# A feed-forward stage: sums of the activations made from a kept scaled input, and the seven-product form begun one hidden tile earlier

## The reference

```python
def rms_norm(x):
    xf = x.astype(jnp.float32)
    return (xf * lax.rsqrt(jnp.mean(xf * xf, -1, keepdims=True) + RMS_EPS)).astype(x.dtype)

def swiglu(h, w_in, w_out):
    gate, up = jnp.split(h @ w_in, 2, axis=-1)
    return (jax.nn.silu(gate) * up) @ w_out
...
        h2 = rms_norm(x) * (1 + sc2) + sh2
        x = x + g2 * swiglu(h2, w_ffn_in[i], w_ffn_out[i])
```

## Time and profile before

| | |
|---|---|
| median of three runs | 2867.03 us |
| the profiled execution | 2864.24 us |
| its span, first to last instruction | 2862.4 us |
| TensorE busy | 2773.7 us, 97% of the span |
| VectorE, ScalarE, GpSimd busy | 1547.7, 918.8, 952.4 us |
| feed-forward from the end of tile 1 | 2192.9 us to the end |
| granted TensorE clock, mean | 0.993 of full |

### The profile page before, as it was taken

How to read it: one execution, slowest core, us unless ns; L and a number is a source line. 1 busy time by engine, 2 the same in 40 slices (tenths; PEclk the granted TensorE clock), 3 DMA queues, 4 the chain that set the end, 5 groups by cost and what they waited for, 6 DMA issues and landing times.

```text
span 2862.4 us, 60609 instructions
## 1 busy us (share of the span) xinstructions
PE 2773.7 (97%) x25599; PEld 2316.0 (81%) x25599; DVE 1547.7 (54%) x1682; ACT 918.8 (32%) x1380; POOL 952.4 (33%) x667
## 2 busy tenths in 40 slices
PE   5999999999999999999999999999998899999999
PEld 4797979898988888887877777888886688888887
DVE  5655555545454646477875666566657633333333
ACT  5312121313131313145454777111122232233322
POOL 1403040404030303044442111333336565566652
PEclk9999999999999999999999999999998999999999
DMA  6202020202020201043331212466311112112122
GB/s 213 67 21 60 21 67 13 75 6 77 3 77 13 67 18 53 18 144 112 121 92 49 60 51 69 149 214 196 114 48 44 30 55 63 45 44 60 50 62 80
DMA packets 224700, 201.93 MB, mean 71 GB/s; under 512 B 22370, under 2 KB 193468, under 8 KB 224444
## 3 DMA queue, kind: packets, MB, share of 16 engines
q1 hardware_dynamic: 210976, 150.70, 17.7%
q10 hardware_dynamic: 13467, 47.31, 4.7%
HBM read 167.57 MB, written 30.41 MB: 69 GB/s over the span
## 4 chain that ended last, share of the span: by engine, by line
PE 91%; DVE 3%; POOL 2%; issue 2%; ACT 2%; DMA 1%; SPq 0%; ACTq 0%; POOLq 0%; DVEq 0%
PE ps L295 67%; PE ps L1052 3%; PE ps L1066 3%; PE ps L1063 2%; PE ps L1030 2%; PE ps L1115 1%; PE ps L1252 1%; PE ps L1277 1%; PE ps L1020 1%; PE ps L1265 1%; PE ps L986 1%; PE ps L1089 1%; PE ps L1099 1%; PE ps L1118 1%; PE ps L1072 1%
## 5 line engine op out<-in xcount | busy, mean ns | idle before, releaser
L295 PE MATMUL ps<-x_hi,w_hi 128*128 128x512 f32 (+1 forms) x2240 | 751.7, 399 | 15.1 <-ACT arena L1953 13.1
L295 PE MATMUL ps<-x_lo,w_hi 128*128 128x512 f32 (+1 forms) x2240 | 733.5, 391 | 0.0
L295 PE MATMUL ps<-x_hi,w_lo 128*128 128x512 f32 (+1 forms) x2240 | 733.5, 391 | 0.0
L285 POOL CAST w_hi<-w_raw 128x1024 fp32r<-128x1024 f32 (+2 forms) x163 | 152.0, 933 | 1532.1 <-PE ps L295 1291.4
L295 PEld LDWEIGHTS ps<-x_hi,w_hi 128*128 128x128 f32 (+1 forms) x2240 | 413.7, 188 | 118.8 <-issue 20.7
L295 PEld LDWEIGHTS ps<-x_hi,w_lo 128*128 128x128 f32 (+1 forms) x2240 | 420.2, 188 | 91.4
L295 PEld LDWEIGHTS ps<-x_lo,w_hi 128*128 128x128 f32 (+1 forms) x2240 | 420.7, 188 | 87.7
L287 POOL TENSOR_TENSOR w_lo<-w_raw,w_hi 128x1024 fp32r<-128x1024 f32 (+2 forms) x163 | 335.4, 2058 | 13.0
L295 PE MATMUL ps<-hid,w_hi 128*128 128x512 f32 (+1 forms) x928 | 259.3, 399 | 12.5 <-DVE arena L2614 9.5
L295 PEld LDWEIGHTS ps<-hid,w_hi 128*128 128x128 f32 (+1 forms) x928 | 172.4, 190 | 56.8 <-issue 12.7
L2614 DVE SCALAR_TENSOR_TENSOR arena<-ps,mod,arena 128x1024 f32<-128x1024 f32 x88 | 112.8, 1284 | 122.1 <-PE ps L295 122.0
(11 more groups left out here) (329 smaller groups left out, 4262.9 us busy)
## 6 DMA issues: line engine op xcount, KB each, us to landing
w_raw<-in_w_in SPq DMA_DIRECT2D x78, 512.0 KB, 3.9
arena<-in_w_ada SPq DMA_DIRECT2D x48, 512.0 KB, 5.9
w_raw<-in_w_ffn_in SPq DMA_DIRECT2D x44, 512.0 KB, 3.8
arena<-gates_sig ACTq DMA_DIRECT2D x40, 512.0 KB, 4.2
gates_sig<-arena ACTq DMA_DIRECT2D x24, 512.0 KB, 2.7
w_raw<-in_w_ffn_out SPq DMA_DIRECT2D x22, 512.0 KB, 3.8
arena<-in_x SPq DMA_DIRECT2D x16, 512.0 KB, 6.5
y_a<-arena ACTq DMA_DIRECT2D x10, 512.0 KB, 2.6
```

What stands on the lines that cost most here:

```text
L285: nc.gpsimd.tensor_copy(hi, raw).then_inc(s_whi, 1)
L295: ins = nc.tensor.matmul(dst[h], wp, xp[h], start=first and m == 0, stop=last and m == 2, skip_group_check=on)
```

## The change

- `normed` writes all eight channel blocks of the scaled input into `mix` (free by then), which is kept whole, where a two-slot buffer was used in turn. VectorE no longer waits for the slot.
- The sums T1 to T4 are made by VectorE from this kept float32 input, one operation each per channel block (16 operations of 512 elements, in place; the shift `sh2` is added or taken off as a per-channel scalar in the same operation). GpSimd's `x_sum` and VectorE's two- and three-operation forms are gone. The low parts are written over the raw sums (`x_sums` is now a list of 33 places of 512, of which 16 lie on `mix`).
- `FIRST_FAST` is 2: tile 2 takes the seven-product form, and down 0 the piece form. Their weight blocks are no longer split whole by GpSimd; their pieces are split by ScalarE and GpSimd as for all later tiles.
- The first fast tile now waits for the sums one product at a time.
- ScalarE makes the Silu of tile 1 after the high parts of T1 and T2, then two of T3, then pieces 0 to 3 and two of T4; the rest stands behind its first copy out of PSUM (`among_first_snaps`). VectorE makes all 16 sums, ten low parts, and then the hidden product of tile 1.

```diff
-          ("wout0", 4, 2), ("wout1", 4, 2), ("ffn_first", 1, 2), ("ffn", 1, 6)]
+          ("wout0", 4, 2), ("wout1", 4, 2), ("ffn_first", 1, 2), ("ffn", 1, 2)]
...
-FIRST_FAST = 3
+FIRST_FAST = 2
 DOWNS = FF // P // FF_GROUP
-ITEMS = [item for i in range(1, DOWNS - 1) for item in (("up", 2 * i + 1), ("up", 2 * i + 2), ("down", i))]
+ITEMS = [("up", 2), ("down", 0)]
+ITEMS += [item for i in range(1, DOWNS - 1) for item in (("up", 2 * i + 1), ("up", 2 * i + 2), ("down", i))]
...
-        x_sums = sb("x_sums", [P, 3, 2, 4, 512], F32R)
+        x_sums = sb("x_sums", [P, 33, 512], F32R)
...
+        X_HI = {X_T1: (20, 21, 22, 23), X_T2: (16, 17, 18, 19), X_T3: (27, 32, 8, 10)}
+        X_LO = {X_T1: (1, 3, 5, 7), X_T2: (9, 11, 13, 15), X_T3: (0, 2, 4, 6)}
...
-            return (0 if q % 2 == 0 else 3), 1, 2
+            gate, other = 2 * SLOT_A, 2 - 2 * SLOT_A
+            return (gate, gate + 1, other) if q % 2 == 0 else (other + 1, gate + 1, other)
...
-            for k in range(4):
-                x_sum(k)
-                split_block(pool, Block("ffn", 2 + k), 1024)
...
-            pool.wait_ge(m_hl, upto(2))
+            pool.wait_ge(m_act, upto(1))
...
             up(Block("ffn", 0), Block("ffn", 1), 1, ready=(m_nh, 0, 1))
-            up(Block("ffn", 2), Block("ffn", 3), 2)
-            down("ffn", 4, 0, 0)
...
                 if q == 0:
-                    pe.wait_ge(m_sil, upto(3))
-                    pe.wait_ge(m_act, upto(3))
+                    pe.wait_ge(m_sil, upto(2))
                 pe.wait_ge(f_h, late(f_h, 2 * (q - 2) + 1))
                 half_product(r0, lambda k: x_quarter(0, k, 0), b1, True)
                 pe.wait_ge(f_post, late(f_post, 3 * (q - 1) + 1))
                 half_product(r0 + 1, lambda k: x_quarter(1, k, 0), d, True)
                 pe.wait_ge(f_snap, late(f_snap, 3 * q + 1))
                 if q == 0:
-                    pe.wait_ge(c_lo, late(c_lo, 12))
+                    pe.wait_ge(c_lo, late(c_lo, 4))
                 half_product(r0 + 2, x_sum_of(X_T2), b1, False)
                 pe.wait_ge(f_post, late(f_post, 3 * (q - 1) + 3))
+                if q == 0:
+                    pe.wait_ge(m_act, upto(2))
+                    pe.wait_ge(c_lo, late(c_lo, 8))
                 half_product(r0 + 3, x_sum_of(X_T1), c, True)
                 pe.wait_ge(f_snap, late(f_snap, 3 * q + 2))
+                if q == 0:
+                    pe.wait_ge(c_lo, late(c_lo, 14))
                 half_product(r0 + 4, x_sum_of(X_T3), b1, False)
...
-            x_sum_high(0)
-            x_sum_high(1)
+            for which in (X_T1, X_T2):
+                for k in range(4):
+                    x_sum_high(which, k)
             hidden(Block("ffn", 0), 1, 1)
-            hidden_high(1, 1)
-            x_sum_high(2)
-            x_sum_high(3)
-            hidden(Block("ffn", 2), 2, 0)
-            last_sum_high(0)
-            last_sum_high(1)
+            for k in range(2):
+                x_sum_high(X_T3, k)
             piece_high(0)
             piece_high(1)
-            last_sum_high(2)
-            last_sum_high(3)
-            act.wait_ge(s_dense, upto(Block("ffn", 5).before + 1))
-            hidden_high(2, 0)
             piece_high(2)
             piece_high(3)
+            for k in range(2):
+                last_sum_high(k)
+
+            def among_first_snaps():
+
+                hidden_high(1, 1)
+                for k in range(2, 4):
+                    x_sum_high(X_T3, k)
+                for k in range(2, 4):
+                    last_sum_high(k)
...
                         if q == 0:
-                            act.wait_ge(m_act, upto(3))
-                            act.wait_ge(c_lo, late(c_lo, 12))
+                            act.wait_ge(m_act, upto(2))
                         else:
                             act.wait_ge(f_h, late(f_h, 2 * q - (1 if j == 0 else 0)))
                         fn({0: s_p1, 2: s_u2, 3: s_p5}[j], ps[:, c if j == 3 else b1, :], ACT.Copy).then_inc(f_snap, 1)
+                        if q == 0 and j == 0:
+                            among_first_snaps()
...
-                    if k >= 1:
-                        dve.wait_ge(m_nh, upto(k))
...
+            def x_sum(which, k):
+
+                n11, n12, n21, n22 = (x_scaled(*q) for q in ((0, k, 0), (0, k, 1), (1, k, 0), (1, k, 1)))
+                sh_0, sh_1 = (mod[:, MOD_SH2 + 4 * h + k:MOD_SH2 + 4 * h + k + 1] for h in range(2))
+                if which == X_T1:
+                    dve.wait_ge(m_nh, upto(KT))
+                    v.tensor_tensor(n12, n12, n11, ALU.subtract).then_inc(c_d, 1)
+                elif which == X_T2:
+                    dve.wait_ge(c_d, late(c_d, k + 1))
+                    v.scalar_tensor_tensor(n22, n22, sh_1, n12, ALU.add, ALU.subtract).then_inc(c_d, 1)
+                elif which == X_T3:
+                    dve.wait_ge(c_d, late(c_d, 4 + k + 1))
+                    v.scalar_tensor_tensor(n11, n22, sh_0, n11, ALU.subtract, ALU.subtract).then_inc(c_d, 1)
+                else:
+                    v.scalar_tensor_tensor(n21, n21, sh_1, n22, ALU.add, ALU.subtract).then_inc(c_d, 1)
+
+            def x_sum_low(which, k, made):
+
+                raw, hi, lo = raw_place(X_LO[which][k]), x_sums[:, X_HI[which][k], :], x_sums[:, X_LO[which][k], :]
+                dve.wait_ge(c_d, late(c_d, ALL_SUMS))
+                dve.wait_ge(c_hi, late(c_hi, made))
+                v.tensor_tensor(lo, raw, hi.bitcast(F32), ALU.subtract).then_inc(c_lo, 1)
...
+            X_T4 = 3
             hidden_low(0, 0)
-            x_sum_low(0)
-            x_sum_low(1)
+            for which in (X_T1, X_T2, X_T3, X_T4):
+                for k in range(4):
+                    x_sum(which, k)
+            for k in range(4):
+                x_sum_low(X_T2, k, 4 + k + 1)
+            for k in range(4):
+                x_sum_low(X_T1, k, k + 1)
+            for k in range(2):
+                x_sum_low(X_T3, k, 8 + k + 1)
             product(Block("ffn", 1), 1, 1)
+            for k in range(2):
+                last_sum_low(k, 10 + k + 1)
             hidden_low(1, 1)
-            x_sum_low(2)
-            x_sum_low(3)
-            product(Block("ffn", 3), 2, 0)
...
+            for k in range(2, 4):
+                x_sum_low(X_T3, k, 12 + k - 1)
+            for k in range(2, 4):
+                last_sum_low(k, 14 + k - 1)
```

More of the change, by code:

```diff
@@ L523, in build @@
         s_fw = [counted_on(s_lw, PAIRS * 96), counted_on(s_mask, 16)]
-        SLOT_A = Block("ffn", 4).slot
+        SLOT_A = Block("ffn", 0).slot
         raw_a, raw_b = w_raw[:, SLOT_A, :], w_raw[:, 1 - SLOT_A, :]
@@ L753, in _ @@
                     if n == 0:
-                        sp.wait_ge(s_wsplit, upto(Block("ffn", 4 + part).before + 1))
+                        sp.wait_ge(s_wsplit, upto(Block("ffn", part).before + 1))
                     elif ITEMS[n - 1][0] == "up":
@@ L1469, in x_sum_of @@
             def x_sum_of(which):
-                return lambda k: (x_sums[:, which, 0, k, :], x_sums[:, which, 1, k, :])
+                return lambda k: (x_sums[:, X_HI[which][k], :], x_sums[:, X_LO[which][k], :])
             def fast_up(tile):
@@ L1956, in hidden_high, with x_sum_high @@
                 act.wait_ge(m_act, upto(tile + 1))
-                fn(hid_hi[:, t, :], ft[:, t, :], ACT.Copy).then_inc(m_hh, 1)
+                fn(hid_hi[:, t, :], hsum, ACT.Copy).then_inc(m_hh, 1)
             hidden_high(0, 0)
-            def x_sum_high(k):
-                act.wait_ge(c_pl, late(c_pl, 6 * k + 3))
-                fn(x_sums[:, X_T1, 0, k, :], raw_t1, ACT.Copy).then_inc(c_hi, 1)
-                act.wait_ge(c_d, late(c_d, 2 * k + 2))
-                fn(x_sums[:, X_T2, 0, k, :], raw_t2, ACT.Copy).then_inc(c_hi, 1)
-                act.wait_ge(c_pl, late(c_pl, 6 * k + 6))
-                fn(x_sums[:, X_T3, 0, k, :], raw_t3, ACT.Copy).then_inc(c_hi, 1)
+            def x_sum_high(which, k):
+                act.wait_ge(c_d, late(c_d, 4 * which + k + 1))
+                if which == X_T3 and k >= 2:
+                    act.wait_ge(c_lo, late(c_lo, 10 + k - 1))
+                fn(x_sums[:, X_HI[which][k], :], raw_place(X_LO[which][k]), ACT.Copy).then_inc(c_hi, 1)
             def last_sum_high(k):
-                act.wait_ge(c_d, late(c_d, 8 + 3 * k + 3))
-                fn(x_quarter(0, k, 1)[0], raw_t4[k % 2], ACT.Copy).then_inc(c_hi, 1)
+                act.wait_ge(c_d, late(c_d, 12 + k + 1))
+                act.wait_ge(s_dense, upto(Block("ffn", 1).before + 1))
+                fn(x_quarter(0, k, 1)[0], x_scaled(1, k, 0), ACT.Copy).then_inc(c_hi, 1)
             def piece_high(r):
@@ L2633, in last_sum @@
-            def last_sum(k):
-                h21, l21 = (t.bitcast(F32) for t in x_quarter(1, k, 0))
-                t2h, t2l = (x_sums[:, X_T2, part, k, :].bitcast(F32) for part in range(2))
-                t = raw_t4[k % 2]
-                n = 8 + 3 * k
```

(10 more changed lines are left out.)

99 lines of the change are left out of this document (16 added, 83 removed).

## The result

| | before | after |
|---|---|---|
| median of 4 runs each, same chip (us) | 2867.04 (2865.82 to 2869.16) | 2846.89 (2843.4 to 2849.4) |
| ratio of the medians, with its 95% interval | | 0.9928 [0.9911, 0.9945] |
| profiled execution: time, span (us) | 2864.24, 2862.4 | 2846.58, 2844.6 |
| mean granted clock of TensorE | 0.993 | 0.997 |

What follows compares the result with a forecast made beforehand. TensorE bounds the kernel, busy 2773.7 of 2862.4 us. End of tile 1 to down 1 takes 92.7 for 112.35, plus 0.6 from tile 1: 20.2 less, 2844.0; with 2.8 for the median, 2846 (range 2838 to 2855).

Steps and rivals of the forecast that it cites:

- twelve matmuls fewer: In tile 2, on TensorE's path: 12 matmuls at 0.2267 us each save 2.7 us, held for certain.
- slot wait: end of tile 1 earlier: VectorE's wait for a slot of `normed` goes, taking 0.6 us off the end of tile 1 (bounds 0 and 1.2).
- a sum, start to start: Each of VectorE's sixteen 512-wide sums takes 0.60 us; upper bound one turn with GpSimd, 1.7.
- end of tile 1's product: VectorE's hidden product of tile 1, behind all 16 sums and ten low parts, ends at 2208.4.
- waits for pieces (half products 1, 2): In tile 2, TensorE waits for GpSimd's low parts of A11 and A12: 1.0 and 0.6 us.
- wait for the copy (half product 3): In tile 2, TensorE idles 9.7 us for ScalarE's copy of a bank, which waits for tile 1's hidden product.
- slow matmuls behind it: In tile 2 behind the copy's wait, 1.7 us lost to the lower clock.
- wait ahead of half product 5: In tile 2, TensorE waits 0.4 us for the second copy, which ends at 2216.7.
- down 0; tiles 3 and 4: Down 0 runs as down 1, 21.76 us, without its 9.5 us of waits; tiles 3 and 4 as 5 and 6, 38.45.
- the short chain: Rival, chance 0.18: VectorE hardly meets GpSimd, 26 operations at 0.60 us ahead of the product; 27 us less, 2840.
- the stall would only have moved: Rival, 0.04 with "not what it says": tile 1's late product makes new waits 28 us or more; 2861 to 2867.
- the kernel become slower: Rival, chance 0.03: VectorE's 26 operations ahead of tile 1's product average over 1.7 us; at 1.95, 2873.

Runs made afterwards that it cites:

- e7: Changed kernel with four more 512-wide VectorE additions ahead of the product of tile 1; tile 2 took 35.95 us against 33.52, single run 2847.01 us.

## Why the prediction was right

2846.0 was forecast and 2846.89 measured. By its own steps (us, measured in the profiled execution):

| step | predicted | measured |
|---|---|---|
| twelve matmuls fewer | 2.7 | 2.7 |
| slot wait: end of tile 1 earlier | 0.6 | 0.2 to 0.3 |
| end of tile 1 | 2192.3 | 2193.11 |
| a sum, start to start | 0.60 | 0.60 (T1), 0.66 (with a scalar) |
| end of tile 1's product | 2208.4 | 2209.40 |
| waits for pieces (half products 1, 2) | 1.0 + 0.6 | 2.65 + 0.41 |
| wait for the copy (half product 3) | 9.7 | 7.84 |
| slow matmuls behind it | 1.7 | 2.5 |
| wait ahead of half product 5 | 0.4 | 0.22 |
| down 0; tiles 3 and 4 | 21.76; 38.45 | 21.76; 38.42 |
| end of tile 1 to down 1 | 92.7 | 93.70 |

**The mechanism held.** Silu is no longer waited for, the wait moved to the product of tile 1 and the copy behind it (lengthened by just what is added to VectorE's list), down 0 has no wait, and twelve matmuls are gone. The long wait is ended by the very chain that was forecast. The rivals fell: VectorE's 26 operations took from 2184.21 to 2208.19, 0.92 us each, between the 0.60 of the short chain and the 1.5 and 1.7 at which the stall would only have moved or the kernel become slower.

**The sizes that were off.** *The wait for the first piece*, 1.0 forecast: GpSimd and VectorE were taken to have a fair turn each from the start; VectorE's back-to-back sums kept GpSimd waiting, 3.14 us in place of 1.29 and some turn. This cost little, because the product's end, not the piece, sets when half product 3 starts: the three waits together are 10.9 us where 11.3 was said. TensorE came to the copy's wait later than forecast, by the longer wait for the piece and by tile 1's end, and so this wait is shorter. *The scalar form* was taken at 0.60 from the 1024-wide row; at 512 it is 0.66, and twelve of them are 0.7 us more. With the sums' start 0.86 later than forecast (2184.21 for 2183.35), this would put the product 1.6 us later; it ended only 1.0 later. The other 0.6 is a slip in the forecast's sum: its own count, two sums and ten low parts, seven of them at 1.7 us and five at 0.60, from 2191.75 on, ends at 2206.65 and not at 2207.2. From the measured start of the last two sums, 2193.25, the same count gives 2208.15, and the product started at 2208.19: the count of the turns was right. *The slow matmuls* were scaled from before (1.7); the 12 matmuls from 2210.14 to 2215.35 take 5.21 us where 2.72 is usual, so 2.5. *The slot wait* is the step that failed: 0.6 us off the end of tile 1 wasn't gained, since the wait was worth 0.2 to 0.3, and in the profiled execution VectorE's second low part sat out GpSimd's split. The forecast didn't look for this; it happens in the kernel before as well and isn't the change's. Waits, slow matmuls and the rest of tile 2 come to 14.5 us; the rows name 13.6, and 0.9 is spread over the matmuls around them.

The windows show the clock, with the columns of the earlier trace rows, after the change:

```profile
2184.00:2206.00 22.00, 15.24 (x65) 11.68 (x64) 21.97 (x25) 10.16 (x17) 12.48 (x7) 0.98 0.00 0
```

TensorE is busy 15.24 of these 22 us (9.04 before) and the granted clock stays at 0.98, near the higher level of 2.4 GHz (0.79 before). It falls only later, behind the 7.84 us of idling (0.50, the lower level of 1.2 GHz, from 2210 to 2215), and then costs about as much as it did behind Silu (2.5 us, before 2.0); what it cost behind down 0's two waits is gone with them.

Part of the agreement is luck: the profiled executions lie 17.7 us apart, and the sum, made against that execution, said 20.2 (2844.0, where 2846.58 was measured). The stretch gave 18.65 of 19.65 forecast in it. The forecast then added 2.8 us for the median, as before; here the median lies 0.3 above the profiled execution, and the two errors nearly cancel. The medians are of 4 runs each, with 3.3 and 6.0 us between their lowest and highest.

Of the duration of 691 ns that the Trainium skill (VectorE: DVE Perf Modes, the part on the errata and the cycle tables) gives for a float32 tensor-by-tensor operation of 512 elements, no extra time came: the trace after the change has T1's four sums in 2.49 us, which is 3 x 0.60 and one duration of 0.68, and e7's four the same. The row decided rightly.

## What to carry to other kernels

When a long wait is to be removed, ask what else ends as late as the thing waited for: Silu moved alone and the product moved alone won nothing, because the list of work behind each was as long, and only taking work out of GpSimd's chain helped. And give a cheaper algorithm whose inputs take long to prepare a plain tile as cover: seven products save 2.7 us per tile, but in the first tile that could use them they cost 14.5, and the same sums with a plain tile 2 were 8 to 10 us faster.

## What the runs showed of the hardware

VectorE and GpSimd operations of 512 elements that read SBUF take turns at 1.74 us for both, whatever the form on VectorE (13.57 and 13.77 us for ten) and with or without waits between them. Not expected: a run of VectorE operations queued back to back can keep GpSimd out over several of them (3.14 and 2.89 us for an operation of 1.29), and a wait ahead of each, for the end of the one before, gives GpSimd back its 1.29 us. The version with seven products from tile 3 on shows it on a cast of a weight block, which takes 1.04 us elsewhere in the same trace and 4.68 beside T3's and T4's sums:

```profile
2193.16 4.68 POOL L285 CAST w_hi<-w_raw 128x1024 fp32r<-128x1024 f32 x1 [6.53 <-issue]
```

The Trainium skill (SBUF — State Buffer, Who interferes with whom) says that the two engines share a pair of ports under an exclusive lock, that a VectorE instruction with two SBUF inputs contends with a GpSimd instruction that reads SBUF, and that the order of issue decides who blocks. The turns of the low parts agree with that, and so do the two pictures of tile 1; that a waiting GpSimd instruction can sit out several queued VectorE instructions is what these rows add.

Who goes first in T4 changed no total, with the same work on both: tile 2 took 33.52 us with GpSimd kept out of T4 and 33.46 with it let in. In tile 1 it did count: without the slot wait, TensorE waited 2.4 us there where GpSimd's split came first and 0.7 where VectorE's low part did.
